# Four activations of the down projection are split ahead of the last two up tiles, and GpSimd makes low parts

## What is computed

```python
up, f_new = causal_dwconv(rmsnorm(h, g_ffn) @ w_up, f_buf, w_fconv)
a, g = jnp.split(up, 2, axis=-1)
y = h + (jax.nn.silu(g) * a) @ w_down
```

## Time and profile before

| | us |
|---|---|
| three runs | 1182.1, 1194.11, 2566.13 (median 1194.11) |
| the profiled execution | 1200.31 |
| its span, first to last instruction | 1198.5 |
| PE busy | 1080.7 (90%) |
| DVE busy | 609.5 (51%) |
| ACT busy | 396.4 (33%) |
| POOL busy | 124.7 (10%) |

### The profile page before, as it was taken

How to read it: one execution, slowest core, us unless ns; L and a number is a source line. 1 busy time by engine, 2 the same in 40 slices (tenths; PEclk the granted TensorE clock), 3 DMA queues, 4 the chain that set the end, 5 groups by cost and what they waited for, 6 DMA issues and landing times.

```text
span 1198.5 us, 19449 instructions
## 1 busy us (share of the span) xinstructions
PE 1080.7 (90%) x7897; PEld 960.8 (80%) x7897; DVE 609.5 (51%) x1273; ACT 396.4 (33%) x746; POOL 124.7 (10%) x174
## 2 busy tenths in 40 slices
PE   3899999899988885989778899999999999899995
PEld 2699999888866553657444799999999999799995
DVE  3534824434233446666576534657676756842231
ACT  3313421333211121453566422433323332522222
POOL 4000020001000001000374100000010001000000
PEclk9999999999868886898899999999999999899998
DMA  7522052543321115162400322222223221222312
GB/s 191 187 71 71 1 200 71 227 177 105 126 90 38 38 38 212 61 246 74 152 1 1 139 72 72 73 73 73 73 93 110 87 73 50 68 72 74 96 48 79
DMA packets 87467, 113.99 MB, mean 95 GB/s; under 512 B 17975, under 2 KB 78489, under 8 KB 85040
## 3 DMA queue, kind: packets, MB, share of 16 engines
q1 hardware_dynamic: 81327, 70.34, 19.5%
q0 software_dynamic: 6080, 42.83, 9.5%
HBM read 103.06 MB, written 13.59 MB: 97 GB/s over the span
## 4 chain that ended last, share of the span: by engine, by line
PE 80%; DVE 10%; ACT 4%; DMA 2%; issue 2%; SPq 0%; ACTq 0%; POOL 0%; DVEq 0%; PEldq 0%
PE banks L1414 12%; PE banks L1412 10%; PE banks L950 6%; PE banks L1449 6%; PE banks L897 5%; PE banks L1448 5%; PE banks L900 4%; PE banks L901 4%; PE banks L934 2%; PE banks L1367 2%; PE banks L1366 2%; PE banks L1115 1%; PE banks L849 1%; PE banks L1045 1%; PE banks L1190 1%
## 5 line engine op out<-in xcount | busy, mean ns | idle before, releaser
L1414 PE MATMUL banks<-xnT_r,RB_r 128*128 128x320 f32 x352 | 109.7, 312 | 0.0
L1414 PE MATMUL banks<-xnT_r,ring_r 128*128 128x320 f32 x352 | 109.4, 311 | 0.0
L1412 PE MATMUL banks<-xnT_r,RB_r 128*128 128x256 f32 x352 | 103.2, 293 | 0.0
L1412 PE MATMUL banks<-xnT_r,ring_r 128*128 128x256 f32 x352 | 98.8, 281 | 0.0
L950 PE MATMUL banks<-RA,RB 128*128 128x128 f32 (+1 forms) x576 | 83.8, 291 | 5.9 <-DVE RA L1667 3.8
L950 PEld LDWEIGHTS banks<-RA,RB 128*128 128x128 f32 x576 | 76.3, 203 | 9.9 <-DVE RA L1667 5.4
L1414 PE MATMUL banks<-RC_r,RB_r 128*128 128x320 f32 x264 | 82.3, 312 | 0.0
L1412 PE MATMUL banks<-RC_r,RB_r 128*128 128x256 f32 x264 | 74.2, 281 | 0.0
L2046 DVE TENSOR_TENSOR ring_r<-ring,RB_r 128x2048 fp32r<-128x2048 f32 x22 | 49.4, 2288 | 38.1 <-ACT RB_r L755 38.1
L1412 PEld LDWEIGHTS banks<-xnT_r,RB_r 128*128 128x128 f32 x352 | 67.0, 190 | 1.2
L1412 PEld LDWEIGHTS banks<-xnT_r,ring_r 128*128 128x128 f32 x352 | 67.6, 192 | 0.0
(11 more groups left out here) (576 smaller groups left out, 2940.6 us busy)
## 6 DMA issues: line engine op xcount, KB each, us to landing
ring<-in_w_up_dram SPq DMA_DIRECT2D x22, 1024.0 KB
ring<-in_w_down_dram SPq DMA_DIRECT2D x8, 1408.0 KB, 7.0
ring<-in_w_in_dram SPq DMA_DIRECT2D x9, 1024.0 KB, 5.5
RB<-in_state_win_dram SPq DMA_DIRECT2D x8, 512.0 KB, 7.1
out_win_s_dram<-in_state_win_dram POOLq DMA_DIRECT2D x1, 4032.0 KB, 23.0
xsp<-RC SPq DMA_DIRECT2D x1, 2304.0 KB, 12.5
xT<-xsp SPq DMA_DIRECT2D x1, 2304.0 KB, 14.4
RA<-in_x_prompt_dram SPq DMA_DIRECT2D x4, 512.0 KB, 5.7
```

The costliest lines, as they stand in the source:

```text
L1412: t.matmul(ps[4 + par][:, w * UA:(w + 1) * UA], wk[:, w, k, c], x[:, 0:UA], skip_group_check=True, **first)
L1414: last = t.matmul(ps[2 * par + w][:, 0:UB], wk[:, w, k, c], x[:, UA:T], **on)
```

## The change

Four activations, k = 8, 9, 0 and 1 (the first four of a new list `FIRST`, which sets the order of the activations on ACT, DVE and PE), are split ahead of tile 20's part on ACT and DVE. For this, `ahi[0]` and `ahi[1]` get homes in half 1 of `ring`, and `hst`, which lay there, goes to `xnT`. Activations at places 12 and 13 of the list (k = 12 and 13), and the whole low part of pass 1's weight slab, are made by POOL in place of DVE. ACT splits that slab's high part inside tile 21, in front of the activations at places 14 to 17. PE waits for the activations in the order of `FIRST`.

```diff
--- before.py
+++ after.py
@@ -256,9 +256,13 @@
         dhi = [[where[:, P * k:P * (k + 1)] for _, n, where in runs for k in range(n)] for runs in dhi_runs]
         ahi = [xhi[:, k, :] for k in range(8)] + [hot[:, k, :] for k in range(8)] + \
               [RB_r[:, T * k:T * (k + 1)] for k in range(6)]
+        for n in range(2):
+            ahi[n] = ring_r[:, 1, 2816 + T * n:2816 + T * (n + 1)]
+        POOL_LO = (12, 13)
+        FIRST = [8, 9, 0, 1] + list(range(2, 8)) + list(range(10, NFF))
         alo = [RC_r[:, T * k:T * (k + 1)] for k in range(NFF)]
         assert len(ahi) == NFF and 6 * T == 3456
-        hst = ring[:, 1, 2816:2816 + 2 * T].rearrange("p (s t) -> p s t", s=2)
+        hst = xnT[:, 0:2, :]
         gB = ktT[:, :, :].rearrange("p s t -> p (s t)")[:, 0:D]
         sqs = kcT_s
         ssy = sb("ssy", [P, NTILE, KD])
@@ -476,6 +480,17 @@
                     A["state_win"][0, :, TS:WIN].rearrange("b r k h d -> b (r k h d)"))
             pool.sem_inc(S("u_fof"), 1)
             for q in range(NFF):
+                if q == NFF - 1:
+                    for n in POOL_LO:
+                        at = FIRST[n]
+                        pool.wait_ge(S("a_hi"), n + 1)
+                        g.tensor_tensor(alo[at], actT[:, at, :], ahi[at].bitcast(F32), ALU.subtract).then_inc(S("wo_lo"), 1)
+                    pool.wait_ge(S("d_hi"), 2)
+                    for k0, n, where in dhi_runs[1]:
+                        last = g.tensor_tensor(dlo[1][:, k0:k0 + n, :].rearrange("p k n -> p (k n)"),
+                                               draw[1][:, k0:k0 + n, :].rearrange("p k n -> p (k n)"), where.bitcast(F32),
+                                               ALU.subtract)
+                    last.then_inc(S("d_lo"), 1)
                 pool.wait_ge(S("u_fo"), q + 2)
                 cols = slice(q * P, (q + 1) * P)
                 pool.dma_start(O["fconv_p"][0, 0].rearrange("j (w n) -> j w n", w=2)[:, :, cols], fo[0:2]).then_inc(S("u_fos"), 16)
@@ -797,9 +812,22 @@
                 act.wait_ge(S("u_act"), k + 2)
                 a.activation(ahi[k], actT[:, k, :], ACT.Copy).then_inc(S("a_hi"), 1)
 
+            act.wait_ge(S("u_mm"), 20)
+            for k in FIRST[0:4]:
+                act_hi(k)
             up_act(0, 20, lambda: split_down_act(0, 16))
-            up_act(1, 21, lambda: [act_hi(k) for k in range(12)])
-            for k in range(12, NFF):
+            act.wait_ge(S("u_mm"), 22)
+            for k in FIRST[4:8]:
+                act_hi(k)
+            def behind_taps():
+                for k in FIRST[8:14]:
+                    act_hi(k)
+                split_down_act(1, 16)
+                for k in FIRST[14:18]:
+                    act_hi(k)
+
+            up_act(1, 21, behind_taps)
+            for k in FIRST[18:]:
                 act_hi(k)
 
 
@@ -822,7 +850,6 @@
                 last.then_inc(S("d_sq"), 1)
 
             act.sem_inc(S("d_sq"), 1)
-            down_act(0, 0, 16, True, False)
             with act.Fori(0, 3) as it:
                 for x in range(2):
                     down_act((1 + x) % 2, it * 2 + (1 + x), it * 16 + (32 if x == 0 else 32), True, True)
@@ -1438,13 +1465,17 @@
                 pe.wait_ge(S("d_lo"), mn + 1)
                 if not first:
                     pe.wait_ge(S("d_add"), mn + 1)
-                for k in range(NFF):
+                for q in range(NFF):
+                    k = FIRST[q]
                     if first:
-                        pe.wait_ge(S("a_lo"), k + 1)
-                        if k == 8:
+                        if q in POOL_LO:
+                            pe.wait_ge(S("wo_lo"), 8 + q - POOL_LO[0] + 1)
+                        else:
+                            pe.wait_ge(S("a_lo"), q + 1 - sum(n < q for n in POOL_LO))
+                        if q == 8:
                             last_cols(21)
                     for n, (w, x) in enumerate(((dhi[s][k], ahi[k]), (dhi[s][k], alo[k]), (dlo[s][:, k, :], ahi[k]))):
-                        on = dict(start=(k == 0 and n == 0), stop=(k == NFF - 1 and n == 2))
+                        on = dict(start=(q == 0 and n == 0), stop=(q == NFF - 1 and n == 2))
                         t.matmul(ps[s][:, 0:UA], w, x[:, 0:UA], **on)
                         last = t.matmul(ps[2 + s][:, 0:UB], w, x[:, UA:T], **on)
                 last.then_inc(S("d_mm"), 1)
@@ -2141,14 +2172,19 @@
                                            ALU.subtract)
                 last.then_inc(S("d_lo"), 1)
 
-            def act_lo(k):
-                dve.wait_ge(S("a_hi"), k + 1)
+            def act_lo(n):
+                k = FIRST[n]
+                dve.wait_ge(S("a_hi"), n + 1)
+                if n in POOL_LO:
+                    return
                 v.tensor_tensor(alo[k], actT[:, k, :], ahi[k].bitcast(F32), ALU.subtract).then_inc(S("a_lo"), 1)
 
+            for n in range(4):
+                act_lo(n)
             up_dve(0, 20, lambda: split_down_dve(0, 0))
-            up_dve(1, 21, lambda: [act_lo(k) for k in range(12)])
-            for k in range(12, NFF):
-                act_lo(k)
+            up_dve(1, 21, lambda: [act_lo(n) for n in range(4, 18)])
+            for n in range(18, NFF):
+                act_lo(n)
 
             def down_dve(s, mn, split, turned):
                 if split:
@@ -2174,7 +2210,8 @@
 
             dve.sem_inc(S("d_add"), 2)
             dve.sem_inc(S("d_out"), 2)
-            down_dve(0, 0, True, False)
+            down_dve(0, 0, False, False)
+            dve.wait_ge(S("d_lo"), 2)
             dve.wait_ge(S("u_fof"), 1 + NFF)
             dve.wait_ge(S("vec_in"), 15 * 16)
             with dve.Fori(0, 3) as it:
```

## The result

The changed kernel took 1204.72 us (median of 20 runs, 1190.39 to 1210.22), the kernel before 1196.0 us (median of 20). The ratio is 1.0093, with a 95% interval of 1.0056 to 1.0129: slower, and far inside the 2% that counts as no change. The profiled execution took 1201.89 us (span 1200.0).

A forecast was written before the change was run, and what follows sets the result against it. TensorE bounds the kernel except in the gap and pass 0, where it waits for DVE's list. With POOL holding DVE +4.4 us, and a clock fall of 2.0, +6.4 on 1194.1 gives 1200.5 us; range 1182 to 1208.

The forecast's parts named there:

- Part 1: Four low parts before tile 20: they push DVE's list back, the gap before pass 0 stays; gain 0.1 us.
- Part 2: DVE's shorter list in pass 0, as if POOL disturbed nobody: pass 1 would start 1.5 us earlier.
- Part 3: POOL's five subtractions (9.3 us) hold up DVE in pass 0: +4.4 us, +6.4 with the clock's fall.
- The turns: In pass 0, POOL's five subtractions and DVE's instructions alternate, one DVE instruction between two of POOL.
- Whoever issued first: Rule for DVE with two SBUF inputs and POOL reading SBUF: the first issued holds the pair for its whole duration.
- The second fall of the clock: In pass 0, PE's 4.3 us wait for place 18 lets its clock fall again; charged 2.0 us.
- Part 4: The rest, with buffer homes, order and the `fo` store: passes 1 to 7 keep 18.16 us each; cost 0.
- no exclusion: Rival, chance 0.24: in pass 0 only short or broadcast instructions block each other; -1.5 us, 1192.6 us.
- DVE always first: Rival, chance 0.13: DVE runs undisturbed in pass 0, PE waits for POOL's weights before pass 1; +3.2 us, 1197.3 us.
- POOL becomes the bound: Rival, chance 0.07: POOL's five take twice 9.3 us, delaying pass 1; +16 us with the clock, 1210 us.
- what they seem to say: Rival, chance 0.03: early low parts fit DVE's 5.00 us idle time, PE starts pass 0 earlier; -6.2 us, 1187.9 us.

The follow-up runs named there:

- late_four: Changed kernel with the four early low parts on DVE put back inside tile 21; last up transposes to pass 1: 32.54 us, ratio 1.0058.
- in_wait: Changed kernel with DVE's four early low parts moved behind tile 20's pad, into its wait for ACT; last up transposes to pass 1: 29.79 us, ratio 1.0132.
- pool_writes: Changed kernel with POOL's five subtractions replaced by memsets, those low parts left out of the products; last up transposes to pass 1: 25.35 us, ratio 0.9976.
- only_two: Changed kernel with pass 1's weights back on DVE, POOL making only places 12 and 13; last up transposes to pass 1: 26.85 us, ratio 0.9929.
- only_weights: Changed kernel with places 12 and 13 back on DVE, POOL making only pass 1's weights; last up transposes to pass 1: 32.03 us, ratio 1.0024.
- dve_all: Changed kernel with POOL's five subtractions given back to DVE, early four kept; last up transposes to pass 1: 26.76 us, ratio 1.0074.
- pool_idle: Changed kernel with POOL making only places 0 to 3, in DVE's idle time before tile 20; last up transposes to pass 1: 24.08 us, ratio 1.0009.
- in_wait_dve: Changed kernel with the early four in DVE's wait for ACT and POOL's subtractions back on DVE; last up transposes to pass 1: 24.07 us, no ratio.
- fill_gap: in_wait_dve with pass 0 summed in banks 0 and 4, starting after tile 20's u_pad; last up transposes to pass 1: 24.50 us, ratio 0.9961.
- pieces: fill_gap with places to 20 split before tile 21's convolution, pass 1 starting on its first weight piece; last up transposes to pass 1: 21.81 us, ratio 0.9968.

## Why the prediction was right

- **Part 1, the early four gain nothing at the start.** PE's start moved from 5.84 to 5.57 us behind the last up transposes; forecast was a gain of 0.1 us, it was 0.27. The clock fell in the gap again. It cost 2.7 us, where I had left it at the 2.0 of before; PE's waits at places 17 and 18 hid the difference. Shown also from the other side: late_four and in_wait move the start to 4.00 and 2.90 us.
- **Part 2, what DVE alone would have given.** Forecast 25.9 us without interference (-1.5); pool_writes gave 25.35.
- **Part 3, POOL holds DVE.** POOL's instructions, less their waits, took 1.3, 1.45, 2.8, 1.4 and 2.0 us, 9.0 in all, against 9.3. The turns came as written for the last three. For the first two they didn't: POOL's first was issued at 1036.05 us, half a us ahead of DVE's next low part, and that one still went first, so that both of POOL's fell into DVE's wait for ACT and cost almost nothing (only_two: 0.1 us). "Whoever issued first" therefore doesn't describe this place, and why it doesn't stays open: in only_weights POOL's first, issued 0.5 us ahead of DVE's place 14 while DVE was idle, did go first. Place 18 therefore came 0.7 us earlier than I had it, PE going on 27.8 us behind the transposes and not 28.5.
- **The second fall of the clock** cost 1.9 us against 2.0. It made the stretch +5.44 in place of +6.4; the difference is the 0.7 us of the turns, and a tenth each in the clock, the last slabs and the rounding.
- **Part 4.** Passes 1 to 7 didn't change.
- **The whole time.** 1200.5 was forecast and 1204.72 measured. Of the 4.2 us between them, 1.9 are the kernel before, whose median I had from three runs (1194.1 for 1196.0). The medians differ by 8.7 us for a stretch of +5.4; the rest fits the share of the two groups, which I had taken into the range and not into the sum, but isn't shown to be that. Three of the four rivals had times inside my range of 1182 to 1208 us too: it is the stretch, and not the whole time, that tells them apart.

The rivals: "no exclusion" is out (the rows above, and dve_all against the changed kernel). "DVE always first" is out for the weights, though it describes POOL's first. "POOL becomes the bound" is out: its weights were there at 1048.1 us, 10.8 us before pass 1. The early four could have done what they seem to say: with in_wait's one-line move, PE does start 2.7 us earlier, and even then the clock falls (below).

## What to carry to other kernels

Work given to GpSimd isn't off DVE's list while both read two operands from SBUF: here 6.2 us of POOL's subtractions cost DVE 6.1 us (three low parts of 0.75 us took 3.51, 2.12 and 2.68) and saved it 3.2. The same subtractions cost nothing where DVE waits anyway (pool_idle), so place them by where DVE idles, and not by how long DVE's list is. And before moving work ahead, look for a wait in front of its new place: idle time that lies before a wait can't be filled from behind it.

A DVE instruction that reads PSUM need not be held. The kernel before has one short case, in its attention stage:

```profile
604.32 1.27 POOL L473 TENSOR_TENSOR ring_r<-ring,RC_r 128x512 fp32r<-128x512 f32 x1
...
604.53 0.43 DVE L1949 TENSOR_TENSOR banks<-banks,causal 128x256 f32<-128x256 f32 x1 [1.28 <-PE banks L1239]
...
608.94 0.43 DVE L1949 TENSOR_TENSOR banks<-banks,causal 128x256 f32<-128x256 f32 x1 [2.53 <-PE banks L1239]
```

DVE's instruction with one operand in PSUM takes 0.43 us beside POOL's subtraction (604.32 to 605.59 us), and 0.43 us at 608.94 us, where POOL is idle. No run here shows it for long instructions.

## What I hadn't expected of the hardware

I had read from the trace before that TensorE's clock falls 2.8 us into an idle time. In in_wait_dve PE idled for only 2.52 us, and the fall came after it had restarted: PE started at 1037.20 us at full clock (2.4 GHz), ran so for more than 1 us, and then did some 3.4 us at 1.2 GHz (0.50 in the rows below). In fill_gap the clock was 1.00 through an idle time of 3.61 us and fell some 0.7 us behind PE's restart (0.60 from 1049 to 1050 us, restart at 1048.53). In pieces PE idled 2.22 us, and the clock was 0.87 in the us of the restart and 0.50 in the next; behind the idle 0.34 us at place 4 it stayed at 1.00.

```profile
1037.00:1038.00 1.00, 0.80 (x6) 0.81 (x7) 0.97 (x6) 0.82 (x2) 0.00 (x0) 1.00 1.14 338
...
1038.00:1039.00 1.00, 1.00 (x8) 1.00 (x8) 1.00 (x3) 1.00 (x2) 0.00 (x0) 0.82 1.17 310
...
1039.00:1040.00 1.00, 1.00 (x6) 1.00 (x5) 1.00 (x2) 1.00 (x3) 0.00 (x0) 0.50 1.16 289
...
1042.00:1043.00 1.00, 1.00 (x9) 1.00 (x9) 1.00 (x3) 1.00 (x2) 0.00 (x0) 0.97 0.12 41
```
